# Inverse roots of nine norms over tokens: square root on ScalarE and reciprocal on VectorE, or addition and power on GpSimd

## The reference, cut to what matters

```python
def rms_norm(x, gain):
    xf = x.astype(jnp.float32)
    y = xf * lax.rsqrt(jnp.mean(xf * xf, axis=-1, keepdims=True) + RMS_EPS)
    return (y * gain.astype(jnp.float32)).astype(x.dtype)
...
        x = x + rms_norm(merged @ w_out[layer], g_mix_post[layer])
        h = rms_norm(x, g_ffn_pre[layer])
        gate, up = jnp.split(h @ w_gate_up[layer], 2, axis=-1)
        x = x + rms_norm((jax.nn.silu(gate) * up) @ w_down[layer], g_ffn_post[layer])
        ple_gate = jax.nn.sigmoid(rms_norm(x, g_ple_pre[layer]) @ w_ple_gate[layer])
        e = (p[layer].astype(x.dtype) @ w_ple_proj[layer]) * ple_gate
        x = x + rms_norm(e, g_ple_post[layer])
```

## Time and profile before

| | |
|---|---|
| median of 3 runs | 2644.96 us (2644.27 to 2646.93) |
| the profiled execution | 2645.49 us, its span 2643.7 us |
| TensorE busy (PE) | 2625.5 us, 99% |
| VectorE, ScalarE, GpSimd busy | 1864.5 us, 1503.2 us, 38.8 us |
| mean granted clock of TensorE | 0.999 of full speed, the 2.4 GHz level |
| sum over a half on VectorE (L1755), 8 times | 154 ns |
| square root of 128x1 on ScalarE (L1234), 8 times | 296 ns |
| reciprocal of 128x1 on VectorE (L1761), 8 times | 158 ns |
| roots by token (L1239 and L1771), 5 times each | 287 ns and 156 ns |

### The profile page before, as it was taken

One profiled execution on the slowest core, in us unless ns is written; L12 is line 12 of the kernel. 1 busy time (PEld: TensorE's weight loads), 2 busy tenths in 40 slices (PEclk: granted clock), 3 DMA queues, 4 the chain that ended last, 5 costly groups with the idle time before them and its releaser, 6 DMA issues.

```text
span 2643.7 us, 38462 instructions
## 1 busy us (share of the span) xinstructions
PE 2625.5 (99%) x13622; PEld 2223.6 (84%) x13622; DVE 1864.5 (71%) x3525; ACT 1503.2 (57%) x2987; POOL 38.8 (1%) x56
## 2 busy tenths in 40 slices
PE   9999999999999999999999999999999999999998
PEld 7888888888888888888887888888888888888887
DVE  7877566565876567657757678766688768866875
ACT  7675555455655455545546665554566546655654
POOL 0000000000000000000003000000000000000000
PEclk9999999999999999999999999999999999999999
DMA  8454547665555665565555555544555665555554
GB/s 281 149 165 162 182 149 239 194 206 191 191 187 187 212 200 187 191 193 189 186 183 187 170 163 188 169 159 166 178 183 192 192 190 191 186 191 191 190 191 160
DMA packets 136816, 493.07 MB, mean 187 GB/s; under 512 B 15704, under 2 KB 16216, under 8 KB 135856
## 3 DMA queue, kind: packets, MB, share of 16 engines
q1 hardware_dynamic: 134064, 480.04, 56.0%
q0 software_dynamic: 2272, 10.31, 1.2%
q10 hardware_dynamic: 288, 0.26, 0.0%
HBM read 488.44 MB, written 4.21 MB: 186 GB/s over the span
## 4 chain that ended last, share of the span: by engine, by line
PE 96%; DMA 1%; DVE 1%; ACT 0%; issue 0%; SPq 0%; DVEq 0%; ACTq 0%
PE bank L607 95%; DMA raw<-in_ws_mix 1%; PE bank L646 0%; DVE lo L1589 0%; DVE X L1592 0%; PE bank L722 0%; DVE arena L1589 0%; ACT sq_t L1154 0%; ACT hi L1049 0%; DVE XS L1592 0%; PE bank L883 0%; PE bank L851 0%; PE bank L670 0%; DVE arena L1592 0%; DVE arena L1596 0%
## 5 line engine op out<-in xcount | busy, mean ns | idle before, releaser
L1589 DVE TENSOR_TENSOR lo<-raw,hi 128x512 fp32r<-128x512 f32 x1804 | 1233.2, 691 | 660.5 <-ACT hi L1049 549.5
L1049 ACT CAST hi<-raw 128x512 fp32r<-128x512 f32 x1804 | 1098.6, 619 | 708.4 <-PE bank L607 689.3
L607 PE MATMUL bank<-XS,hi 128*128 128x512 f32 x3632 | 1000.5, 397 | 1.4 <-DVE XS L1592 1.4
L607 PEld LDWEIGHTS bank<-XS,hi 128*128 128x128 f32 x3632 | 621.5, 189 | 91.8 <-issue 3.8
L607 PEld LDWEIGHTS bank<-XS,lo 128*128 128x128 f32 x3632 | 557.6, 189 | 77.5
L607 PE MATMUL bank<-XS,lo 128*128 128x256 f32 x3632 | 578.5, 281 | 0.0
L607 PE MATMUL bank<-hi,HS 128*128 128x512 f32 x1968 | 551.0, 391 | 0.0
L607 PE MATMUL bank<-hi,XS 128*128 128x512 f32 x1600 | 447.8, 394 | 2.8 <-DVE XS L1592 1.2
L607 PEld LDWEIGHTS bank<-hi,HS 128*128 128x128 f32 x1968 | 366.7, 188 | 75.8 <-ACT hi L1049 1.3
L607 PEld LDWEIGHTS bank<-hi,XS 128*128 128x128 f32 x1600 | 295.1, 188 | 66.9 <-ACT hi L1049 5.6
L607 PE MATMUL bank<-lo,HS 128*128 128x512 f32 x984 | 324.8, 389 | 0.0
(11 more groups left out here) (197 smaller groups left out, 970.5 us busy)
## 6 DMA issues: line engine op xcount, KB each, us to landing
raw<-in_ws_ffn SPq DMA_DIRECT2D x528, 512.0 KB, 3.5
raw<-in_ws_mix SPq DMA_DIRECT2D x338, 512.0 KB, 3.6
raw<-in_ws_ple SPq DMA_DIRECT2D x35, 512.0 KB, 3.8
arena<-in_gains POOLq DMA_DIRECT2D x4, 1024.0 KB, 7.3
X<-in_xt POOLq DMA_DIRECT2D x1, 2048.0 KB, 13.0
t5rows<-t5row POOLq DMA_DIRECT2D x8, 256.0 KB, 5.0
out<-arena SPq DMA_DIRECT2D x8, 256.0 KB, 2.5
X<-in_x SPq DMA_DIRECT2D x7, 256.0 KB, 4.6
```

The lines of the kernel that those rows point to most:

```text
L607: return eng.matmul(o, l, r, start=start, stop=stop, skip_group_check=True)
L1049: eng.copy(hi[:, b % SPL, :], raw[:, u % RAW, part * BW:(part + 1) * BW]).then_inc(halved.next(b), 1)
L1589: return eng.tensor_tensor(o, a, b, op)
```

## The change

The mean is made by the squares: each is scaled by 1/sqrt(2048) before it is squared. VectorE's sums stay. Root and reciprocal are replaced by two instructions on GpSimd: `tensor_scalar` adds 1e-6 in place, and, after a wait for that, `tensor_tensor` raises the result to the power of -0.5, which stands in two columns of `small`. Whoever waited for VectorE's reciprocal waits for GpSimd's signal `n_pool`. ScalarE loses the 13 roots and the 4 roots of constants.

```diff
@@ square_quarter (ScalarE)
-                eng.activation(junk, src, ACT.Square, accum_out=parts_of(n)[:, m, q:q + 1]).then_inc(t_act.next(key), 1)
+                eng.activation(junk, src, ACT.Square, scale=D ** -0.5, accum_out=parts_of(n)[:, m, q:q + 1]).then_inc(
+                    t_act.next(key), 1)
@@ carried (ScalarE)
-                if name == "mix2":
-                    root_table()
                 for m in range(2):
                     (square_of_wout if name == "ffn" else square_of_down if name == "ple" else square_of_eout)(g, m)
-                    root_of_half(n, m)
@@ root_of_half, root_by_token (VectorE)
             def root_of_half(n, m):
-                on.wait_ge(n_act, (n, "sqrt", m))
-                r = roots_of(n)[:, m:m + 1]
-                eng.reciprocal(r, r).then_inc(n_dve.next((n, "root", m)), 1)
-                on.wait_ge(n_dve, (n, "root", m))
+                on.wait_ge(n_pool, (n, "root", m))
...
@@ gpsimd
+            powers = small[:, 88:90]
+
+            def root_of(n, halves):
+
+                for m in halves:
+                    on.wait_ge(n_dve, (n, "sum", m))
+                    s, r = sums_of(n)[:, m:m + 1], roots_of(n)[:, m:m + 1]
+                    eng.tensor_scalar(s, s, EPS, None, ALU.add).then_inc(n_pool.next((n, "mean", m)), 1)
+                    on.wait_ge(n_pool, (n, "mean", m))
+                    eng.tensor_tensor(r, s, powers[:, m:m + 1], ALU.pow).then_inc(n_pool.next((n, "root", m)), 1)
+
+            def root_by_token(n):
...
+            eng.memset(powers, -0.5).then_inc(n_pool.next("powers"), 1)
+            on.wait_ge(n_pool, "powers")
+            root_by_token("mix")
...
+            root_of("wout", range(2))
...
+            root_by_token("ffn")
...
+            root_of("down", range(2))
             make_rest("ple")
+            root_by_token("ple")
+            root_of("eout", range(2))
+            root_by_token("mix2")
...
+            root_by_token("ffn2")
+            root_of("final", range(2))
```

More of the change, by code:

```diff
@@ L516, in program @@
         t_act, t_dve, n_act, n_dve = signal("t_act"), signal("t_dve"), signal("n_act"), signal("n_dve")
+        n_pool = signal("n_pool")
         crossed, n_pe, wide = signal("crossed"), signal("n_pe"), signal("wide")
@@ L1075, in quarter_of_heads @@
                     yield at - g.last
-                    on.wait_ge(n_dve, ("mix", "root"))
+                    on.wait_ge(n_pool, ("mix", "root"))
                     for m in range(2):
@@ L1098, in quarter_of_values @@
                     o = b_bv[:, :, cut(g.q)]
-                on.wait_ge(n_dve, (n, "root"))
+                on.wait_ge(n_pool, (n, "root"))
                 for m in range(2):
@@ L1153, in square_quarter @@
                 last_square.append(key)
-                eng.activation(junk, src, ACT.Square, accum_out=parts_of(n)[:, m, q:q + 1]).then_inc(t_act.next(key), 1)
-            def root_table():
-                eng.activation(sums_of("final"), const("eps").to_broadcast([P, 2]), ACT.Sqrt).then_inc(n_act.next("table"), 1)
+                eng.activation(junk, src, ACT.Square, scale=D ** -0.5, accum_out=parts_of(n)[:, m, q:q + 1]).then_inc(
+                    t_act.next(key), 1)
             def quarter_of_wout(g):
@@ L1193, in quarter_of_ple @@
                     on.wait_ge(gemm, ("half", g.g, m))
-                    on.wait_ge(n_dve, ("ple", "root"))
+                    on.wait_ge(n_pool, ("ple", "root"))
                     on.wait_ge(in_z, 7)
@@ L1230, in square_of_x @@
                 square_quarter(n, m, q, XT[:, m, cut(q)], (g.g, m))
[L1232 to L1240, removed]
             def value1(g):
@@ L1345, in next_root @@
             def next_root(name):
-                root_by_token(name)
-                if name == "ple":
-                    return
                 yield NORM_AT[name] + (4 if name == "mix" else 1) - ROOT_AT[name]
@@ L1357, in by_its_root @@
                 def by_its_root(m, q):
-                    on.wait_ge(n_dve, ("final", "root", m))
+                    on.wait_ge(n_pool, ("final", "root", m))
                     on.wait_ge(t_dve, ("final", q, m))
@@ L1527, in scalar @@
                 agenda.at(CROSS["ffn2"][c], entered(c))
-            for name in ("mix", "ffn", "ple", "mix2", "ffn2"):
+            for name in ("mix", "ffn", "mix2", "ffn2"):
                 agenda.at(ROOT_AT[name] + 1, next_root(name))
             agenda.at(plan.ticks - 2, final())
-            for g in (by["wout", 2], by["down1", (2, 2)], by["down2", (2, 2)]):
-                agenda.at(g.last + 4, tables())
             agenda.at(13, squares())
@@ L1769, in root_by_token @@
             def root_by_token(n):
-                on.wait_ge(n_act, (n, "sqrt"))
-                eng.reciprocal(roots_of(n), roots_of(n)).then_inc(n_dve.next((n, "root")), 1)
-                on.wait_ge(n_dve, (n, "root"))
+                on.wait_ge(n_pool, (n, "root"))
             def gained(g, k, m, after):
@@ L2438, in make_rest @@
                     t.then_inc(filled.next((name, s)), 1)
+            powers = small[:, 88:90]
[7 more added lines that the diff above has]
+            def root_by_token(n):
+                on.wait_ge(n_dve, (n, "sum"))
+                eng.tensor_scalar(sums_of(n), sums_of(n), EPS, None, ALU.add).then_inc(n_pool.next((n, "mean")), 1)
+                on.wait_ge(n_pool, (n, "mean"))
+                eng.tensor_tensor(roots_of(n), sums_of(n), powers, ALU.pow).then_inc(n_pool.next((n, "root")), 1)
+            eng.memset(powers, -0.5).then_inc(n_pool.next("powers"), 1)
+            on.wait_ge(n_pool, "powers")
+            root_by_token("mix")
             on.wait_ge(h_pe, (1, "turned", 1))
```

5 lines of the change are left out of this document (removed).

## The result

The changed kernel took 2648.34 us (median of 20 runs, 2646.17 to 2649.90), the kernel before 2644.97 (20 runs beside it, 2643.37 to 2646.99): ratio 1.0013, 95% interval 1.0007 to 1.0019, so 3.4 us more. The forecast was 2649.3. The profiled execution took 2648.26, its span 2646.2, 2.5 over the span before.

The account below looks back on a forecast made before the run. TensorE, holding 96% of the span, bounds the kernel, except where it waits for roots through VectorE and ScalarE. Terms 1.0 + 1.5 + 1.5 + 0.5 - 0.1 = +4.4 us on 2644.96 give 2649.3 us, range 2645 to 2660.

Parts of the forecast that it names:

- S: Time from the end of VectorE's sum to a usable root: 0.53 us before, forecast 1.1 us on GpSimd.
- c: Extra arithmetic of a power on GpSimd over a plain one-column instruction, taken as 0.35 us, at most 1.7.
- wout: End of `wout`: first root 0.57 us later, second 0.4, together +1.0 us.
- down: End of `down`: first root 0.57 us later, second 0.9 as it waits for the gain product, together +1.5 us.
- TensorE itself is 1.5 late: Last chunks before `ple`: GpSimd's rest of the residual 2.3 us late, covered by TensorE's lateness and 1.9 slack; no wait.
- eout: End of `eout`: the lost table load's gain eaten by two roots one behind the other, +0.5 us, bounds -0.7 and +3.3.
- End of the program: Last three scalings and the stores behind them come later, same queue order as in `down`: +1.5 us.
- Start: `mix` root ready at 43.3 instead of 44.86; given -0.1 us, bounds -0.9 and 0.
- Contention: `down`, program's end: GpSimd's addition waits for VectorE's two-SBUF-input gain product, not in `wout`; without this the sum is 3.0 us.
- slow power: Rival, GpSimd's roots: a power's extra arithmetic is 1 us or more, program 2656.5 us or 2660.5; chance 0.36.
- first use: Rival, program start: GpSimd's first power loads code; 4 us makes 2651.8 us, the skill's 6 us 2653.8; chance 0.08.
- freed engines: Rival: roots take 0.55 us, `eout` gains 0.7, the start 0.9; sum -0.8, 2644.2 us; chance 0.06.

Follow-up runs that it names:

- e_power_twice: The changed kernel with each power of the four norms by half made twice, one after the other; 2654.07 us, ratio 1.0032 to the kernel before.
- e_rest_vector4: The changed kernel with VectorE making four instead of three of the eight residual steps ahead of the ple norm; 2649.76 us, ratio 1.0015 to the kernel before.
- e_scale_first: The changed kernel with GpSimd's first scaling of the rest of the residual moved ahead of down's second root; 2647.97 us, ratio 1.0013 to the kernel before.
- e_gain_behind: The changed kernel with VectorE's second-half gain product behind its wait for the root in wout and down; 2648.66 us, ratio 1.0017 to the kernel before.
- e_no_addition: The changed kernel without GpSimd's addition of 1e-6 and its wait in the four norms by half; 2645.81 us, ratio 1.0001 to the kernel before.

## Why the prediction was nearly right

- **S** was put at 1.1 and is 1.00 where nothing runs beside it: the addition 0.22 (forecast 0.26), the power 0.57, so c is 0.37 over the 0.20 of a plain instruction (forecast 0.35). Two scalings of 384 columns in 2.47 are 1.24 each and not 1.25, so a column is 2.5 ns and 0.28 is left for one column; the sum doesn't feel it.
- **`wout`**, +1.0, is +0.7: S was put 0.1 too high in both halves.
- **`down`** was mis-sized, +1.5 against +1.9. Its first transpose is 1.25 late. The other 0.6 is the rest of the residual. The step that failed: "TensorE itself is 1.5 late ... If GpSimd were held up by 1.1 us more, TensorE would wait." I count from VectorE's first sum in `down` (1401.36 against 1400.76), so 0.60 less than the rows say. GpSimd's first addition to the residual was then 2.1 late (1407.58 against 1404.92), 0.2 better than I had it. But its steps ran 1.7 longer beside VectorE, so that it ended 3.8 late. And TensorE came to the last chunks not late at all: its transpose would have started at 1426.63, 0.46 behind the matmuls ahead of it (1426.17) as in the chunks before, against 1425.97 in the earlier trace rows. It had made up some 1.2, most of it where the kernel before has its wait at 1413.23 (0.50 by the profile). So GpSimd's 3.8 less the slack of 1.9 is how late that transpose is; less the 1.2 that TensorE had made up, some 0.6 are left. I had named a wait at these chunks as a sign of being wrong, and it was one.
- **`eout`**, +0.5, is +0.5, made as forecast: counted from ScalarE's sigmoid ahead of it (1501.74 against 1499.16, 2.58 later), the square starts 0.6 and the sum 0.25 earlier, the first root is held by the gain product, and the second pair stands behind it.
- **End of the program**, +1.5: the scalings are 1.1 late, but from there to the end it takes 0.5 less, +0.6 in all. I had taken the stores to follow one for one. Why G is shorter was not tried; it also varies by 0.5 among the kernels with the old order there.
- **Start**, -0.1, is -0.7, near the bound of -0.9. My reason against it, that casts already wait for TensorE, did not hold: the wait in front of the transposes goes as a whole in all three profiles of the changed kernel. But that is not certain: eight more profiles have the same start, and in three of them the wait is there, 0.20 (e_power_twice), 0.33 (e_rest_vector4) and 1.18 (e_scale_first), this last more than in any profile of before. In e_scale_first a cast had waited 1.48 for its weights (42.40), so this term goes with their arrival too. The root itself was mis-sized: S is 1.79 there and not 1.1, both of its instructions being held beside VectorE's low halves. It still came 0.44 before that of the earlier trace rows, because ScalarE's table load ahead of the root (41.96, 1.28 us) is gone.
- **Contention** as forecast, and e_gain_behind shows it. The Trainium skill, page "SBUF — State Buffer", section "Who interferes with whom", lets a GpSimd instruction that reads SBUF wait for a VectorE instruction with two inputs there that came first; the runs agree, with 0.22 alone, 0.59 and 0.72 beside it, and 0.22 in `wout`, where an input is in PSUM. The power in e_no_addition, started beside the product, ends 0.4 after it.
- **Rivals.** The slow power is out (570 ns). The first use is not dear: the first power, at 43.42, ends 0.59 after VectorE's low half beside it (43.83), just as the later one at 684.16 does (685.38 against 684.79). The freed engines pay 0.7 at the start in the mean of three and 0.3 at `eout`, not enough.

So the terms were off by +0.4 (`down`), -0.3, -0.6 and -0.9 (`wout`, start, end), and make 3.0 in place of 4.4; the runs say 3.4, with an interval of 1.9 to 5.0.

## What to carry to other kernels

A step on a chain costs its hand-over as much as its work: here an addition of one number, 0.3 to 0.8 us with its hand-over, eight times, was worth nearly the whole loss on balance, and at `eout` it rode in a sum that was made anyway. Move a small step to an idle engine where nobody waits for it, not because the engine is idle. A new wait costs what is left after the waits that it makes vanish: 1.69 in the profile was 0.6, and taking it away by loading VectorE gained nothing.

## What the hardware showed beyond that

A power of 128x1 on GpSimd takes 0.57 us. For 128x2 the median is 1.21, but that is not its own length. In the changed kernel the five stand like these two:

```profile
1432.20 0.69 DVE L1563 TENSOR_TENSOR lo<-raw,hi 128x512 fp32r<-128x512 f32 x1 [0.35 <-ACT hi L1050]
1432.26 1.22 POOL L2425 TENSOR_TENSOR cols<-cols,small 128x2 f32<-128x2 f32 x1
```
```profile
1914.10 0.73 POOL L2425 TENSOR_TENSOR cols<-cols,small 128x2 f32<-128x2 f32 x1
1914.39 0.69 DVE L1563 TENSOR_TENSOR lo<-raw,hi 128x512 fp32r<-128x512 f32 x1 [0.70 <-ACT hi L1050]
```

Three start 0.05 or 0.06 behind VectorE's low half, whose two inputs are in SBUF, and take 1.21 or 1.22; so does the first, in part. The one that starts ahead of it takes 0.73, so one more column costs some 0.16 us, and the other 0.49 is the wait for VectorE. There the low half, started 0.29 behind the power, keeps its 0.69. That does not fit the rule as the prediction gives it, by which whoever comes first has the ports for its whole length. VectorE can be held as well: in the profile of before its low half at 1405.97 takes 1.23 for 0.69, beside GpSimd's additions to the residual (1404.92 to 1406.64).

In e_gain_behind VectorE's product was not lengthened by GpSimd's scaling, started 0.04 earlier by the profile, while the scalings were (2.66 for 2.14). By the same section of the Trainium skill it is the order of issue that decides who waits; these rows show the first to start as the one that waits, and at 0.04 us apart they can't tell who was first in truth.
